# Two-layer block kernel: a fourth seven-product pair in each w_ff1, one read for two parts, and the turn a slab later

## The reference, cut to what matters

```python
def squared_relu_mlp(h, w1, w2):
    z = jax.nn.relu(h @ w1)
    return (z * z) @ w2
...
        x = x + squared_relu_mlp(rms_norm(x, ffn_norm[i]), w_ff1[i], w_ff2[i])
```

## Time and profile before

| | |
|---|---|
| median of 3 runs | 2959.76 us (2959.05 to 2961.48) |
| the profiled execution | 2960.76 us, its span 2959.0 us |
| mean granted TensorE clock | 0.998 |
| matmuls | 12996 |
| reads and writes of HBM | 598.89 MB and 10.49 MB |

### The profile page before, as it was taken

How to read it: one execution, slowest core, us unless ns; L and a number is a source line. 1 busy time by engine, 2 the same in 40 slices (tenths; PEclk the granted TensorE clock), 3 DMA queues, 4 the chain that set the end, 5 groups by cost and what they waited for, 6 DMA issues and landing times.

```text
span 2959.0 us, 35189 instructions
## 1 busy us (share of the span) xinstructions
PE 2916.3 (99%) x12996; PEld 2400.2 (81%) x12996; DVE 2055.5 (69%) x2679; ACT 1616.3 (55%) x2134; POOL 634.5 (21%) x1257
## 2 busy tenths in 40 slices
PE   8999999999999999999999999999999999999998
PEld 7888888888888778788788888888888887878887
DVE  6547777777866777876777777756557777887555
ACT  6435555555554566755555555545444446775433
POOL 0003312213043310013203122133324663100210
PEclk9999999999999999999999999999999999999999
DMA  7546777778777655556777778776876776666774
GB/s 263 165 151 203 237 248 250 246 244 255 243 223 243 205 170 164 164 174 203 228 256 253 251 242 253 246 219 211 239 216 200 219 227 190 207 206 206 249 254 157
DMA packets 358156, 649.53 MB, mean 220 GB/s; under 512 B 38624, under 2 KB 63584, under 8 KB 357216
## 3 DMA queue, kind: packets, MB, share of 16 engines
q1 hardware_dynamic: 312976, 578.89, 61.7%
q0 software_dynamic: 44432, 67.45, 7.2%
q10 hardware_dynamic: 576, 0.94, 0.1%
HBM read 598.89 MB, written 10.49 MB: 206 GB/s over the span
## 4 chain that ended last, share of the span: by engine, by line
PE 73%; DVE 14%; DMA 7%; ACT 4%; issue 2%; DVEq 0%; ACTq 0%
PE acc L2093 21%; PE acc L2095 21%; PE acc L2094 21%; DMA raw<-in_w_ff 6%; DVE wlo L1457 5%; ACT whi L1086 1%; DVE wlo L1450 1%; PE tp L2130 1%; PE tp L2132 1%; PE tp L2131 1%; DVE mkv L1472 1%; DVE ob L1900 1%; PE tp L2299 1%; PE sd L2193 0%; PE sd L2218 0%
## 5 line engine op out<-in xcount | busy, mean ns | idle before, releaser
L1457 DVE TENSOR_TENSOR wlo<-raw,whi 128x1024 fp32r<-128x1024 f32 x920 | 1110.7, 1220 | 548.4 <-ACT whi L1086 544.0
L2093 PE MATMUL acc<-whi,set_hi 128*128 128x512 f32 x3696 | 1459.4, 395 | 20.8 <-DVE wlo L1457 15.4
L2095 PE MATMUL acc<-whi,set_lo 128*128 128x512 f32 x3696 | 1440.3, 390 | 0.0
L2094 PE MATMUL acc<-wlo,set_hi 128*128 128x512 f32 x3696 | 1439.8, 390 | 0.0
L1086 ACT ACTIVATE whi<-raw 128x1024 fp32r<-128x1024 f32 x920 | 959.4, 1057 | 684.1 <-PE acc L2095 378.3
L2093 PEld LDWEIGHTS acc<-whi,set_hi 128*128 128x128 f32 x3696 | 694.8, 188 | 182.8 <-DVE wlo L1457 27.1
L2095 PEld LDWEIGHTS acc<-whi,set_lo 128*128 128x128 f32 x3696 | 694.5, 188 | 146.2
L2094 PEld LDWEIGHTS acc<-wlo,set_hi 128*128 128x128 f32 x3696 | 695.0, 188 | 143.3 <-issue 1.9
L1050 POOL DMA_DIRECT2D u<-u x832 | 406.8, 497 | 1447.5 <-DVE u L1648 1337.9
L1450 DVE SCALAR_TENSOR_TENSOR wlo<-raw,par,whi 128x512 fp32r<-128x512 f32 x160 | 111.7, 747 | 47.1 <-ACT whi L1089 46.3
L1089 ACT ACTIVATE whi<-raw,par 128x512 fp32r<-128x512 f32 x160 | 104.2, 715 | 22.4 <-PE acc L2095 10.9
(11 more groups left out here) (332 smaller groups left out, 2121.3 us busy)
## 6 DMA issues: line engine op xcount, KB each, us to landing
raw<-in_w_ff SPq DMA_DIRECT2D x560, 512.0 KB, 4.7
raw<-in_w_in SPq DMA_DIRECT2D x248, 512.0 KB, 4.5
raw<-in_w_out SPq DMA_DIRECT2D x96, 512.0 KB, 4.4
u<-u POOLq DMA_DIRECT2D x832, 32.0 KB, 4.2
raw<-in_w_mem_kv SPq DMA_DIRECT2D x32, 512.0 KB, 4.3
raw<-in_w_proj_a SPq DMA_DIRECT2D x32, 512.0 KB, 4.7
raw<-in_w_proj_b SPq DMA_DIRECT2D x32, 512.0 KB, 6.9
raw<-in_w_kv SPq DMA_DIRECT2D x48, 256.0 KB, 3.3
```

Of the source, the lines that this page charges most:

```text
L1457: V.tensor_tensor(wlo[:, c], src, whi[:, c].bitcast(f32), ALU.subtract).then_inc(w_lo, 1)
L2093: T.matmul(o, h[:, tok], whi[:, c], start=first, stop=False)
L2094: T.matmul(o, h[:, tok], wlo[:, c], start=False, stop=False)
L2095: ins = T.matmul(o, l[:, tok], whi[:, c], start=False, stop=last)
```

## The change

A layer gets four pairs, PAIRS = (0, 1, 1, 2): chunk 0 none, chunks 1 and 2 one each, chunk 3 two, so that chunk 3 has no plain group of w_ff1 and its w_ff2 follows directly on that of chunk 2. The two pairs of chunk 3 stand one after the other around f, the first slab of chunk 2's w_ff2: the first over slabs f - 21 to f + 5, the second over f + 6 to f + 29. Of p3 and p6, the parts now alternate, and p6 has no read: its chain_sum takes p3's block from raw, and SP waits for that sum before it reads into the place again. Odd pairs use the PSUM banks in another order. The turn of a group hangs one slab behind its square. The last two groups of chunk 2's w_ff2 and the first two of chunk 3's are woven in new orders. Where the diff is cut, "..." stands; what is left out hands bank(p, stage) and pair.col on.

```diff
         p = len(self.pairs)
-        pair = Pair(layer, chunk, src, not any(q.layer == layer for q in self.pairs))
+        pair = Pair(layer, chunk, src, col, not any(q.layer == layer for q in self.pairs))
         self.pairs.append(pair)
...
@@ -155,7 +155,7 @@
                     taken[t.slot] += SLAB_K if self.groups[of].pieces else 1
                 else:
                     part.n = t.n
-                    taken[t.slot] += part.stage != "p1"
+                    taken[t.slot] += part.stage not in ("p1", "p6")
                 t.loads = taken[t.slot]
                 self.stream.append(t)
         self.number = {NSLAB * t.g + t.s: t.n for t in self.stream if t.part is None}
...
@@ -294,9 +294,14 @@
 
 
 FF2_PAIR = ((0, 1, 2, 3, 4, 5), (6, 7))
-
-
-STAGES = ("p1", "p2", "p5", "p3", "p6", "p7", "p4")
+FF2_LATE = ((0, 1, 2, 3), (4, 5), (6, 7))
+FF2_EVEN = ((0, 1), (2, 3), (4, 5), (6, 7))
+
+
+PAIRS = (0, 1, 1, 2)
+
+
+STAGES = (("p1",), ("p2",), ("p5",), ("p3", "p6"), ("p7",), ("p4",))
 CHAIN = {"p1": 0, "p5": 1, "p6": 2, "p4": 3}
 BLOCKS = {"p1": (0, 0), "p2": (1, 0), "p5": (0, 1), "p3": (1, 1), "p6": (1, 1), "p7": (0, 0), "p4": (1, 0)}
 SUMS = {"p5": 0, "p7": 1, "p3": 2, "p6": 3}
...
 
+    def seven(layer, chunk, src, col, first, last):
+
+        p = sc.pair_of(layer, chunk, src, col, first, last)
+        pair = sc.pairs[p]
+        sc.at("act", pair.end("p1") + 5, "part_p1", p)
+        sc.at("dve", pair.end("p2") + 3, "part_c11", p)
+        sc.at("act", pair.end("p5") + 3, "part_p5", p)
+        sc.at("dve", pair.end("p6") + 3, "part_q", p)
+        return p
+
+    def drain(p, of, rst, z, kt, turn, split):
+
+        pair = sc.pairs[p]
+        add = pair.end("p7") + 3
+        if of == "n1":
+            add = max(pair.end("p4") + 3, add + 5)
+        sc.at("dve", add, "part_" + of, p)
+        sc.at("act", add + 2, "relu_" + of, p, rst)
+        sc.at("act", add + 2, "part_square", p, of, sc.staged, sc.tails)
+        sc.turned(max(turn, add + 3), split, ("staged", sc.staged), z, kt)
+        sc.staged += 1
+        if of == "n2":
+            sc.at("act", add + 3, "part_p7", p, sc.staged)
+
     def ffn(layer, rst, a, z, next_rst, next_gain):
 
-        for c in range(NCHUNK):
-            halved = c > 0
-            gs = [sc.group(f"w_ff1{layer}", 0, D * c + GW * i, a) for i in range(2 if halved else 0, 4)]
+        waiting = []
+        for c, count in enumerate(PAIRS):
+            gs = [sc.group(f"w_ff1{layer}", 0, D * c + GW * i, a) for i in range(2 * count, 4)]
             if c == 0:
                 sc.fed_late(gs[0])
                 v = S * gs[0]
@@ -386,39 +415,36 @@
                 for n in range(4):
                     sc.at("act", v + (13, 14, 16, 17)[n], "sum_hi", layer, n)
                     sc.at("dve", v + (14, 15, 17, 18)[n], "sum_lo", layer, n)
-            else:
+            elif count == 1:
                 v = S * gs[0]
-                pair = sc.pairs[p]
-                for of, kt, add, square, turn, split in (
-                        ("n2", 0, pair.end("p7") + 3, pair.end("p7") + 6, pair.end("p7") + 6, v + 1),
-                        ("n1", 4, pair.end("p4") + 3, pair.end("p4") + 6, v + 2, v + 9)):
-                    sc.at("dve", add, "part_" + of, p)
-                    sc.at("act", add + 1, "relu_" + of, p, rst)
-                    sc.at("act", square, "part_square", p, of, sc.staged, sc.tails)
-                    sc.turned(turn, split, ("staged", sc.staged), z, kt)
-                    sc.staged += 1
-                    if of == "n2":
-                        sc.at("act", square + 1, "part_p7", p, sc.staged)
+                p, = waiting
+                drain(p, "n2", rst, z, 0, f + 11, v + 1)
+                drain(p, "n1", rst, z, 4, v + 2, v + 9)
             for i, g in enumerate(gs):
-                turn, split = S * (g + 1) + 1, S * (g + 2) + 1
-                if halved:
-                    turn, split = S * (g + 1) + 2, S * (g + 2) + 2
-                sc.at("act", S * (g + 1) + 1, "epi_relu2", g, rst, sc.staged, sc.tails)
-                sc.at("act", turn, "epi_square", g, sc.tails)
-                sc.turned(turn, split, ("staged", sc.staged), z, 4 * i + (8 if halved else 0))
+                e = S * (g + 1)
+                late = 1 if count else 0
+                sc.at("act", e + 1, "epi_relu2", g, rst, sc.staged, sc.tails)
+                sc.at("act", e + 1 + late, "epi_square", g, sc.tails)
+                sc.turned(e + 2 + late, e + 9 + late, ("staged", sc.staged), z, 4 * (2 * count + i))
                 sc.staged += 1
             fs = [sc.group(f"w_ff2{layer}", D * c, GW * i, z) for i in range(4)]
-            sc.weave(fs[0], fs[1], FF2_PAIR)
-            if c < NCHUNK - 1:
-                v = S * fs[0]
-                p = sc.pair_of(layer, c + 1, a, v - (14 if halved else 12), v + 26)
-                pair = sc.pairs[p]
-                sc.at("act", pair.end("p1") + 3, "part_p1", p)
-                sc.at("dve", pair.end("p2") + 3, "part_c11", p)
-                sc.at("act", pair.end("p5") + 3, "part_p5", p)
-                sc.at("dve", pair.end("p6") + 3, "part_q", p)
-            for n, left in ((0, 2), (4, 1), (12, 0)):
+            f = S * fs[0]
+            sc.weave(fs[0], fs[1], FF2_PAIR if count < 2 else FF2_LATE)
+            at_need = ((0, 2), (4, 1), (12, 0)) if count < 2 else ((0, 3), (2, 2), (8, 1), (12, 0))
+            for n, left in at_need:
                 sc.groups[fs[n // S]].need[n % S] = [("tail_lo", sc.tails - left)]
+            more = PAIRS[c + 1] if c < NCHUNK - 1 else 0
+            if more == 1:
+                waiting = [seven(layer, c + 1, a, 0, f - (11, 14, 2)[count if c else 0], f + 26)]
+            elif more == 2:
+                sc.weave(fs[2], fs[3], FF2_EVEN)
+                first, middle = (f - 21, f + 6) if c else (f - 11, f + 9)
+                p = seven(layer, c + 1, a, 0, first, middle - 1)
+                q = seven(layer, c + 1, a, 2 * GW, middle, f + 29)
+                drain(p, "n2", rst, z, 0, f + 11, f + 23)
+                drain(p, "n1", rst, z, 4, f + 24, f + 29)
+                drain(q, "n2", rst, z, 8, f + 31, f + 37)
+                drain(q, "n1", rst, z, 12, f + 38, f + 44)
             for i, g in enumerate(fs):
                 e = sc.end(g)
                 sc.epilogue(g, "add", GW * i)
...
@@ -681,7 +707,12 @@
         acc = [ctx.enter_context(nc.psum_tensor(f"acc{i}", [P, TB * GW], f32)) for i in range(2)]
         tp = ctx.enter_context(nc.psum_tensor("tp", [P, 4 * TOK], f32))
         sd = ctx.enter_context(nc.psum_tensor("sd", [P, 4 * TOK], f32))
-        bank_a, bank_b, bank_c, bank_d = tp[:, 0:GW], tp[:, GW:2 * GW], sd[:, 0:GW], sd[:, GW:2 * GW]
+        quarters = tp[:, 0:GW], tp[:, GW:2 * GW], sd[:, 0:GW], sd[:, GW:2 * GW]
+
+        def bank(p, stage):
+
+            n = {"p1": 0, "p6": 0, "p4": 0, "p2": 1, "p7": 1, "p5": 2, "p3": 3}[stage]
+            return quarters[(2, 3, 1, 0)[n] if p % 2 else n]
 
         def gain_of(gain, kt):
 
...
@@ -882,9 +913,16 @@
 
         @block.sync
         def _(sp):
+            def shared_block(task):
+
+                before = sc.stream[task.n - RAW].part if task.n >= RAW else None
+                if before and before.stage == "p3":
+                    sp.wait_ge(sm["chain_add"], QUARTERS * (3 * before.pair + CHAIN["p6"] - 1) + before.j + 1)
+
             def slab(task):
                 of, k, _, _ = sc.slab_of(task.g, task.s)
                 of = sc.groups[of]
+                shared_block(task)
                 if task.n >= RAW:
                     sp.wait_ge(w_lo, task.n + 1 - RAW)
                 dst = raw[:, task.slot * SLAB:(task.slot + 1) * SLAB]
@@ -902,6 +940,8 @@
 
             def part_load(task):
                 part = task.part
+                if part.stage == "p6":
+                    return
                 if part.stage == "p1":
                     pair = sc.pairs[part.pair]
                     if pair.first:
...
                     sp.dma_start(in_rows(chain_raw[part.j]), block_of(part, "p1"))\
                         .then_inc(sm[f"chain_in{part.j}"], 16)
                     return
+                shared_block(task)
                 sp.wait_ge(w_lo, task.n + 1 - RAW)
                 sp.dma_start(in_rows(raw[:, task.slot * SLAB:(task.slot + 1) * SLAB]), block_of(part, part.stage))\
                     .then_inc(ld[task.slot], 16)
...
 
                 act.wait_ge(mm, sc.pairs[p].last("p1"))
-                A_(first_c[:], bank_a, ACT.Copy).then_inc(sm["part_p1"], 1)
+                if p:
+                    act.wait_ge(sm["part_relu"], 2 * p)
+                A_(first_c[:], bank(p, "p1"), ACT.Copy).then_inc(sm["part_p1"], 1)
 
...
@@ -1465,10 +1508,13 @@
 
             def chain_sum(task):
 
+                part = task.part
+                if part.stage == "p6":
+                    task = sc.stream[sc.pairs[part.pair].parts["p3", part.j].n]
```

(45 more changed lines are left out.)

## The result

The changed kernel takes **2976.93 us** in the median of four executions (2974.57 to 2980.16), the one before, measured with it, 2959.63 (2959.05 to 2961.48): 1.0059 times the time before, 95% interval 1.0043 to 1.0075. So it is slower by some 17 us, where 2958.0 was forecast with a range of 2949 to 2975. The profiled execution took 2974.87 us, 14.1 more than the profiled one before.

What follows compares the result with a forecast made beforehand. Two limits were named: DVE's work and the loop through the read, with TensorE busy 99%. Terms -10.9 + 9.4 + 1.0 - 1.3 = -1.8, from the profiled 2960.8 less 1.0 for the median, gave 2958.0 us, range 2949 to 2975.

Steps and rivals of the forecast that it cites:

- Step 1: Pairs in both layers: 28 parts (168 matmuls) replace 192 matmuls, a fourth pair a layer, -10.9 us in all.
- Step 2: Reads for p3 and p6: 4 fewer a pair keep the old read rate; SP's wait, 1.14 us, got no term.
- If reads waited long for the shared block's sum: Sign named in advance that the forecast would be wrong: reads held long behind p6's sum; no size given.
- Step 3: Two back-to-back pairs before chunk 3: DVE steps use up the lead, 2.4 and 2.3 us, 4.7 a layer, +9.4.
- rival B: Crowded stretches: the read becomes the bound, two rounds take 9.0 us, 2976 in total; chance 0.24.
- the loop: Freed raw block, read into it, chain sum, x sum, next wlo, then TensorE; priced at 0.1 in p5.
- D: Time from a freed raw block to its sum; taken as 4.7 us, ends seen 3.64 and 6.15.
- the working's own formula: Two rounds of the crowded stretches take D + 3.5 us, against 8.16 us of TensorE.
- Step 4: Turn one slab behind its square: +1.0 in w_ff1's third group, -1.3 at 1471 in layer 1.
- Step 5: Later shuffles, last z tile, ACT's copies, rotated PSUM banks and POOL's turns: all covered, cost nothing.
- A: Crowded stretches: the lead covers everything if D is about 4.2, some 0.3 us a layer left, 2949; chance 0.34.
- C: Stalls gather into gaps that lower TensorE's clock, two or three dips a layer, some 9 us, 2967; chance 0.05.

Runs made afterwards that it cites:

- e4: The changed kernel with p6 reading its own block again and no SP wait for the shared block, 32 reads more: 2988.21 us, 1.0089.
- e7: The changed kernel with three pairs a layer instead of four, PAIRS = (0, 1, 1, 1), all else kept: 2974.90 us, 1.0051.
- e10: The changed kernel with three pairs a layer and e9's rule for raw places, four places: 2959.36 us, 0.9992.
- e9: The changed kernel, four raw places; p1 and p6 hold none, and a read takes the place that came free longest ago: 2961.60 us, 1.0000.
- e1: The changed kernel with five raw places instead of four, attention masks left out to make room: 2947.81 us, 0.9954.
- e2: The kernel before with five raw places instead of four, attention masks left out to make room: 2954.56 us, 0.9974.
- e6: The kernel before with the turns moved one slab on, nothing else: 2960.58 us, 1.0003.
- e5: The changed kernel with the turns put back on the square's own slab, nothing else: 2972.69 us, 1.0042.
- e11: The changed kernel with a fifth raw place over the attention masks in the MLPs, e9's place rule, turns on the square's slab: 2946.02 us, 0.9944.
- e8: The changed kernel with a fifth raw place over the attention masks in the MLPs and turns on the square's slab: 2947.96 us, 0.9959.
- e12: The kernel before with four raw places and e9's place rule, p6 keeping its place since it reads: 2960.04 us, 0.9998.
- e3: The changed kernel, where a part's read into raw brings only its first 128 of 256 rows: 2952.33 us, 0.9967.

## Why the prediction was wrong, step by step

**Step 1 (matmuls, -10.9)** held: 12948 at the old cadence.

**Step 2 (the shared block, at nothing)** failed: its wait stood in the working, but no term of the sum has it. It was priced as "1.14 us later", which holds where p6 is at most two tasks behind p3, as in the crowded stretches: its sum then comes right behind p3's wlo. At the old spacing, two parts in five tasks, p6 stands three tasks behind p3, and its sum only comes behind the wlo of the task after p3. SP waited 2.5 us for it, and the next read with it. That is +5.1 us in chunk 1's w_ff2, which e4 shows to be the wait's doing, and by e7 and e10 some 15 us in a kernel with three pairs. "If reads waited long for the shared block's sum" stood in the prediction as a way to be wrong, without a price; nobody had counted the tasks from p3 to p6 at each spacing. e9 gives back 2.3 us in chunk 0's w_ff2 too, but the kernel before had 2.4 there and e4, without the wait, has 3.9, so this isn't the shared block's.

**Step 3 (crowded stretches, +9.4)** had the mechanism right and one term mis-sized, and by the sections it is the largest miss: +16.5. At the places forecast, f+2 to f+5 and f+24 to f+29, the excess is 4.2 us in each layer, for a forecast of 4.7. The other 3.6 and 4.6 stand almost wholly in the p5 of each pair (693 and 797 in layer 0), where rival B had them and where the forecast let the loop cost 0.1. D was taken as 4.7, the median of all reads to landing. Where DVE waited for a read in these stretches of the changed kernel, D was 5.35 in the mean (26 sums, 4.26 to 6.75); in e9, outside of them, 4.54 (29 sums). By the working's own formula two rounds then take 8.85 against 8.16, a loss of 0.7 where the forecast had 0.04. These are the sums that had to wait, so the long reads are picked: eleven such double rounds would lose more than was measured. The reads as a whole were no slower: their median in layer 0's crowded stretches is 4.6, against 4.7 in that part of the kernel before. But a read that SP asked for within 2 us of the one before took 5.2 us in the mean (72 reads of the crowded stretches of both layers), the others 4.3 (109), and 17 of the 26 sums waited for a read of the first kind.

**Step 4 (the turn, -0.3)** held in half, and its +1.0 was mis-sized. In the first w_ff1 the turn costs 1.4 us a layer where the clock stays (last section), 3.0 in both by e1 against e2, for a forecast of 1.0. The place that was forecast, the third group, is right, with 0.6 in e6; new gaps at the second group, 0.37 us in layer 0 and 0.67 in layer 1 of the changed kernel, were not in the sum. The 1.09 at 1476 is gone, as forecast, and e6 shows that the turn alone does it; but e5, with the turn back, hasn't the gap either. The gaps at p4 in layer 1's w_ff2 grew by 1.0. They are 0.8 over the kernel before in e6 too, where nothing is shared, and longer still in e5; with e9's rule they are gone, but which part of the change lengthened them isn't shown. Over chunk 0's sections e6 has the turn at +1.3, over both MLPs at 0.0, within what its medians can't tell from nothing.

**Step 5 (at nothing)** held: e1, with all of it in place, has at most 0.2 us a section behind the first w_ff1, and e11 0.1 us a layer from chunk 1 on.

In sum, for the profiled executions: -10.9 from step 1, +5.1 for 0 in step 2, +16.5 for +9.4 in step 3, and +3.2 for -0.3 in step 4, 0.9 of it the clock's: +14.

**The rivals.** A, the cover that holds, is what the kernel does with five places; that its price of 2949 is close to 2947.8 and 2948.0 is in part luck, since it was worked out for four and a D of 4.2. With four it was out, since D is over 5.0 in the stretch that counts. B gave 2976 and so hit the time, and its condition, D over 5.0, came true; but it was half luck: the crowded stretches cost 8 us a layer, not 13.7, and the shared block's wait and the first w_ff1 made up the rest. C's clock never fell in a crowded stretch of the changed kernel (1.00 in the rows above); it fell in the first w_ff1, and once each in e7 and e5 behind gaps of 3.1 and 2.1 us further on.

## What to carry to other kernels

When a task stops reading, take its buffer place away too, and count at every spacing how many tasks lie between a block's first user and its last: that distance comes off the read-ahead of everything behind it. When a stretch gets denser, size the read by those that are asked for right behind another, not by the median over the program. And where a chain of buffer, read, sum and product sets the gaps, a place more for the buffer, even one lent for a stretch, can be worth more than the work removed: here, by the ratios of e1 and e2, 8 us for the kernel before and 31 for the changed one.

## What the hardware showed that was not expected

The granted clock after one and the same gap. In each layer, at the third group of the first w_ff1, PE stands 2.0 to 2.2 us. In the kernel before the clock behind it stayed full in layer 0 and fell in layer 1:

```profile
324.00:328.86 4.86, 2.89 (x14) 2.07 (x12) 3.95 (x6) 4.83 (x7) 0.62 (x2) 1.00 0.01 3
328.86:331.58 2.72, 2.72 (x12) 2.24 (x13) 2.72 (x3) 0.34 (x1) 2.72 (x6) 1.00 0.42 92
```

In the changed kernel it fell in both; layer 0:

```profile
324.84:329.61 4.77, 2.89 (x14) 2.07 (x12) 2.91 (x4) 4.74 (x7) 0.00 (x0) 1.00 0.43 129
329.61:334.05 4.44, 4.44 (x13) 3.49 (x13) 4.44 (x5) 1.52 (x2) 1.60 (x4) 0.62 0.43 124
```

A slab took 4.44 us instead of 2.72, part of it at the 1.2 GHz level: 1.72 us. Over the profiled executions of all 14 kernels the clock fell at 14 of the 28 such gaps, with no difference in the gap's length (2.01 to 2.23 us either way) that would tell which.

The 14 kernels also part the clock's share from the turn's. Excess of layer 0's first w_ff1, us:

| | clock stayed | clock fell |
|---|---|---|
| turn on the square's slab | 3.17 to 3.31 (before, e2, e8, e11) | 4.80, 4.81 (e12, e5) |
| turn one slab on | 4.58 to 4.64 (e1, e6, e7, e9) | 5.43 to 5.50 (changed, e3, e4, e10) |

So the turn costs 1.4 us where the clock stays and 0.7 where it falls, and the fall costs 1.6 or 0.9. The two don't add up, because with the turn a slab on PE waits once more behind that slab; in e6:

```profile
332.70 0.50 PE L2093 MATMUL acc<-whi,set_hi 128*128 128x512 f32 x1 [0.40 <-DVE wlo L1457]
```

In the changed kernel, where PE was slow on the slab, there is no such wait. In layer 0 of this comparison the clock stayed before and fell after, in layer 1 it fell in both. So of the 3.3 us lost in the first w_ff1 some 0.9 came with the execution, and 2.4 with the change.
